# The feature tiles of the activations spread by 64 bytes each, in a two-layer hybrid decoder trunk on one core

## The reference

```
h    = rms_norm(x, norm_w[layer])
proj = einsum('bsd,de->bse', h, w_in[layer])        # 4096 -> 11792 columns
y    = concat(gla(...), swa(...), diff(...), rglru(...))   # four mixers of 1024 columns on slices of proj
y    = y * silu(gate)                               # gate: the last 4096 columns of proj
x    = x + einsum('bse,ed->bsd', y, w_out[layer])   # 4096 -> 4096
```

## Time and profile before

| | |
|---|---|
| time, median of 3 runs | 2979.4 us (2978.9 to 2979.46) |
| the profiled execution | 2979.48 us |
| its span | 2977.7 us |
| instructions | 37606 |
| PE (matmul) busy | 2938.4 us, 99% of the span |
| PEld (weight load) busy | 2479.5 us, 83% |
| DVE busy | 1604.9 us, 54% |
| ACT busy | 1458.0 us, 49% |
| bytes moved | 546.68 MB, mean 184 GB/s |

### The profile page before, as it was taken

One profiled execution on the slowest core, in us unless ns is written; L12 is line 12 of the kernel. 1 busy time (PEld: TensorE's weight loads), 2 busy tenths in 40 slices (PEclk: granted clock), 3 DMA queues, 4 the chain that ended last, 5 costly groups with the idle time before them and its releaser, 6 DMA issues.

```text
span 2977.7 us, 37606 instructions
## 1 busy us (share of the span) xinstructions
PE 2938.4 (99%) x14857; PEld 2479.5 (83%) x14857; DVE 1604.9 (54%) x2120; ACT 1458.0 (49%) x2059; POOL 52.0 (2%) x107
## 2 busy tenths in 40 slices
PE   8999999999999999999999999999999999999999
PEld 6888898888888898888878888988888888988887
DVE  5445455555666446444554455555556664554444
ACT  5344445555556545444554434445455665553333
POOL 2000000000000000000000000000000000000000
PEclk9999999999999999999999999999999999999999
DMA  7565556666655666666656655566666556666665
GB/s 223 175 187 161 163 164 174 185 186 181 178 163 162 185 177 190 217 214 203 212 176 191 184 157 169 160 184 181 181 179 177 162 167 180 183 200 207 219 219 168
DMA packets 281889, 546.68 MB, mean 184 GB/s; under 512 B 17688, under 2 KB 21920, under 8 KB 281712
## 3 DMA queue, kind: packets, MB, share of 16 engines
q1 hardware_dynamic: 271472, 524.88, 59.0%
q0 software_dynamic: 5552, 17.26, 1.9%
q10 hardware_dynamic: 4688, 2.13, 0.3%
HBM read 535.81 MB, written 8.39 MB: 183 GB/s over the span
## 4 chain that ended last, share of the span: by engine, by line
PE 98%; DMA 1%; ACT 1%; issue 1%; DVE 0%; ACTq 0%; PEldq 0%; DVEq 0%
PE main L1141 91%; PE mixer L1141 5%; DMA w_raw<-in_w_in 1%; ACT L385 0%; PE mixer L1355 0%; PE mixer L1200 0%; ACT stage L385 0%; PE mixer L1295 0%; PE mixer L1335 0%; PE mixer L1188 0%; DMA mix<-in_norm_w 0%; PE mixer L1322 0%; PE mixer L1285 0%; PE mixer L1323 0%; DVE w_lo L692 0%
## 5 line engine op out<-in xcount | busy, mean ns | idle before, releaser
L1141 PE MATMUL main<-w_hi,act 128*128 128x512 f32 x6912 | 2207.1, 394 | 26.7 <-PE main L1141 13.1
L692 DVE TENSOR_TENSOR w_lo<-w_raw,w_hi 128x1024 fp32r<-128x1024 f32 x992 | 1212.7, 1224 | 1238.8 <-PE main L1141 1004.8
L378 ACT ACTIVATE w_hi<-w_raw 128x1024 fp32r<-128x1024 f32 x992 | 1044.6, 1059 | 1099.5 <-PE main L1141 1076.0
L1141 PEld LDWEIGHTS main<-w_hi,act 128*128 128x128 f32 x6912 | 1299.7, 188 | 314.8 <-issue 39.1
L1141 PE MATMUL main<-w_lo,act 128*128 128x512 f32 x3456 | 1347.7, 390 | 0.0
L1141 PEld LDWEIGHTS main<-w_lo,act 128*128 128x128 f32 x3456 | 650.7, 188 | 129.2
L1141 PE MATMUL main<-act,w_hi 128*128 128x256 f32 x2048 | 377.2, 285 | 3.5 <-PE main L1141 1.8
L1141 PEld LDWEIGHTS main<-act,w_hi 128*128 128x128 f32 x2048 | 321.6, 192 | 6.2 <-issue 5.8
L1141 PE MATMUL main<-act,w_lo 128*128 128x256 f32 x1024 | 289.7, 283 | 0.0
L1141 PEld LDWEIGHTS main<-act,w_lo 128*128 128x128 f32 x1024 | 196.4, 192 | 0.2
L672 DVE SCALAR_TENSOR_TENSOR act<-act_T,par,act 128x256 fp32r<-128x256 f32 x96 | 42.0, 478 | 2.8 <-ACT act L360 2.5
(11 more groups left out here) (250 smaller groups left out, 1126.0 us busy)
## 6 DMA issues: line engine op xcount, KB each, us to landing
w_raw<-in_w_in SPq DMA_DIRECT2D x736, 512.0 KB, 3.6
w_raw<-in_w_out SPq DMA_DIRECT2D x256, 512.0 KB, 3.6
out<-mix POOLq DMA_DIRECT2D x15, 512.0 KB, 3.1
mix<-in_x POOLq DMA_DIRECT2D x8, 512.0 KB, 5.8
mix<-out POOLq DMA_DIRECT2D x8, 512.0 KB, 5.7
mix_Y<-in_x SPq DMA_DIRECT2D x3, 1024.0 KB, 16.3
mix_Y<-in_x SPq DMA_DIRECT2D x2, 512.0 KB, 4.8
act_T<-in_lru_w_r ACTq DMA_DIRECT2D x16, 64.0 KB, 2.0
```

The costliest lines, as they stand in the source:

```text
L378: act.activation(w_hi[:, n % HI, :, :], w_raw[:, n % RAW, :, :], ACT.Copy).then_inc(w_hi_ready, 1)
L692: dve.tensor_tensor(w_lo[:, n % LO, :, :], w_raw[:, n % RAW, :, :], w_hi[:, n % HI, :, :].bitcast(F32), ALU.subtract).then_inc(w_lo_ready, 1)
L1141: return pe.matmul(out_, lhsT, rhs, start=start, stop=stop, skip_group_check=True)
```

## The change

`act` gets feature tiles of 2 x 256 + 16 elements, 2112 bytes, of which the last 64 bytes are not used; `A` is a view of the rest with the same four indices as before, so no other line changes. `pad2` goes. After it, tile k begins at 18432 + 2112 k, `act_T` is at 42 x 2048 and `mix_Y` at 58 x 2048, and `w_raw`, `w_hi`, `w_lo` and all tiles behind them lie 128 bytes higher than before: `w_raw` at 151680, 74 x 2048 + 128.

```
         pad = sb("pad", [P, 56])
-        A = sb("act", [P, KT, 2, SEQ], F32R)
+        A_ROW = 2 * SEQ + 16
+        A = sb("act", [P, KT, A_ROW], F32R)[:, :, 0:2 * SEQ].rearrange("p k (q n) -> p k q n", q=2)
         F = sb("act_T", [P, KT * SEQ])
         YB = sb("mix_Y", [P, 6 * BW + HEADS * (SEQ + 4)])
-        pad2 = sb("pad2", [P, 480])
         w_raw = sb("w_raw", [P, RAW, KG, NC])
```

## The result

The changed kernel takes 3019.4 us (median of four runs, 3016.8 to 3021.0) against 2979.4, a ratio of 1.0134 with an interval of 1.0116 to 1.0151: 40 us slower. The forecast was 2979.4 with a range up to 3000, so the forecast and the range both missed. No engine has another instruction or another order; only addresses differ.

The account below looks back on a forecast made before the run. The prediction took PE's pace through the main matmuls to bound the kernel. Its terms for operand places, line crossings, ACT and DVE, and weight landing summed as 0 + 0 + 0 + 0, leaving 2979.4 us, range 2974 to 3000.

Parts of the forecast that it names:

- What bounds the kernel: Whole kernel: only PE's pace of main matmuls, or a feed so late that PE waits, could move the time.
- The remainder of 13.3 ns a matmul: Main matmuls: what is left of 226.7 ns wide and 120.0 narrow after one column a cycle, the same in both.
- How the two operands lie to each other: Main matmuls: stationary slice's address against the streamed one's, taken as zero, with ends of -13.3 and +4.3 ns.
- the low-rank projection: Nearest row with finer steps: stationary tile steps by 128 bytes, 231 ns a matmul, 4.3 ns above the main pace.
- The streamed row over a 2 KB line: Matmuls whose streamed row crosses a 2 KB line: taken as zero, upper end 11,808 x 4.3 ns = 51 us.
- The slower rival: All ordinary and half of turned chunks: line crossings cost PE time, 9.8 us (2989) to 51 us (3030); chance 0.17.
- The signs asked for in the prediction: PE's pace tile by tile: loss alike for all tiles means the streamed row, loss depending on k means the skew.
- The exception named there: Tiles k = 2, 10, 18 and 26 keep a 512-byte step against the weights, so a skew loss would spare them.
- ACT, DVE and the landing: Splits, act writers and weight transfers: zero each; splits stay 1059 and 1224 ns, no loss under a 6.9 us landing.
- The faster rival: Main matmuls: stationary load and stream stop colliding, 156 us saved, to 2823 us, or 2832 by the skill; chance 0.07.
- The range: Whole kernel: 2974 to 3000 us, holding the 0.75 for no change and crossings of up to 1.7 ns, about 0.1.

Follow-up runs that it names:

- e3_both128: Against the kernel before: everything from act on moved by 128 bytes together, tiles packed; 2980.1 us, ratio 1.0001.
- e10_matched: Against the kernel before: act tile k 64 x (k mod 4) bytes past a multiple of 256, its weight tiles at equal places; 3012.8 us, ratio 1.0113.
- e1_w128: Against the kernel before: act left packed, weights and all behind them moved to 128 bytes past a 2 KB line; 3024.9 us, ratio 1.0154.
- e9_turned64: Against the kernel before: in turned chunks only, w_hi and w_lo written and read 64 bytes further on; 2966.9 us, ratio 0.9959.
- e11_w64: Against the kernel before: act left packed, weights and all behind them moved to 64 bytes past a 2 KB line; 2985.0 us, ratio 1.0018.
- e5_fine_stairs: Against the kernel before: eight blocks of four act tiles at 16 to 240 bytes past a line, weights on 2 KB lines; 3017.9 us.
- e8_planes: Against the kernel before: act stored as two planes, high parts and low parts, without any gap, weights on 2 KB lines; 2979.9 us, ratio 0.9999.
- e12_step256: Against the kernel before: act tile k at 256 x (k mod 8) bytes past a 2 KB line, weights on 2 KB lines; 2979.4 us, ratio 0.9999.
- e4_stairs: Against the kernel before: four blocks of eight act tiles at 0, 64, 128 and 256 bytes past a line; 3004.1 us, ratio 1.0083.

## Why the prediction was wrong, point by point

**What bounds the kernel: right.** PE's pace was the only thing that could move it, and did. The remainder of 13.3 ns a matmul, read off the two paces, is the quantity that the places change: 13.3 ns over the streamed columns at place 0, 20 at place 64 in ordinary chunks (233.3), 6.7 in the best turned ones (113.3).

**How the two operands lie to each other: the step that failed.** "I take zero for this part" rested on a pace that is the same in all positions of the kernel before. But all of these are multiples of 512 bytes, and the effect has a period of 256: all rows of before, many as they are, showed one case. The only row with finer steps, the low-rank projection, showed 4.3 ns more, and I argued it away by its 32 columns. The price itself was in reach: 10,368 x 4.3 = 45 us, against the 40 measured. It stood at the end of the range of this step and was then given to no rival of its own, only lent to the crossing. What the runs show in place of the zero is a pace that depends on the two operands' places modulo 256 bytes: 5.0 ns more for a wide matmul and 1.2 less for a narrow one.

The low-rank row was also read a little high. Start by start, its two narrow matmuls take 0.26 us together and not 0.24, and the 31 wide ones are 230.0 ns apart, 230.8 in the second layer: 3.3 and 4.1 ns more than the main pace, or 34 and 43 us for 10,368. That these lie on both sides of 40 is partly chance, since the row has other places than the changed kernel. But in the kernel before its matmuls are already 224 to 239 ns apart in an uneven pattern, where the main ones keep 226 or 227, and a mean over 31 hid it. The row's stationary tile steps by 128 bytes in every run, so its slices never have one place, and it is above 226.7 in every run: 230.0 and 230.8 in e3_both128, 228.7 and 228.9 in the changed kernel. That is what one would expect if it is the same effect, but no run placed `wa` in steps of 256 bytes, so it isn't shown.

**The streamed row over a 2 KB line: right to cost it at zero.** e3_both128 shows it. The slower rival, with 0.17 of the chance, was this one, and it named the wrong mechanism; its 3030 at 4.3 ns came near by accident. The signs asked for in the prediction told them apart: it had a loss that depends on k for the skew, and the pattern over four tiles is there. The exception named there (none at k = 2, 10, 18, 26) isn't: the matmuls of tile 6, at an equal place modulo 256, are 228, 233 and 230 ns apart in chunk 28. The neighbours' places count as well, as e10_matched shows.

**ACT, DVE and the landing: right.** 1059, 1225, 495 and 478 ns, and 3.6 us to land with w_raw 128 bytes past a line. By the Trainium skill, "DMA: Bandwidth & Descriptors", section "How a descriptor splits into AXI transactions", an estimate of 3.8 us stood beside it; neither the changed kernel nor e1_w128 shows it, both at a median of 3.6.

**The faster rival: wrong sign, with something in it.** Equal places are the best for wide streams, not the worst. For narrow ones they are among the worst, and e9_turned64 takes 12.8 us from that. The rival's limit by the Trainium skill, "TensorE: Matmul & The Clock Gate", section "Wait — 56ns, not 53.3ns?", 215.7 ns for 512 columns, was reached at no place: 226.7 is the lowest of twelve.

**The range.** It stopped at 3000 with the slower case priced at up to 3030. The prediction gave 0.18 to that side and then left nearly half of it outside.

## What to carry to other kernels

A kernel that is bound by PE's pace, with a weight load for each matmul in float32r, should have the distance between its stationary and streamed tiles checked modulo 256 bytes, and every change of a tile's size ahead of them as well: here 16 bytes off cost up to 3% of a wide matmul's time in most chunks, and padding by multiples of 256 cost nothing. For narrow matmuls other places were better than equal ones, so the place is worth trying out for each kind. A pace that is equal at all positions proves nothing about positions that the kernel doesn't have; look first at the step between those that it has. When one row disagrees with the argument and its price can be multiplied out, that price deserves a rival of its own.

## What the runs showed of the hardware that was not expected

- With a weight load ahead of each matmul in float32r, the distance from one matmul to the next depends on the addresses of both operands modulo 256 bytes: 226.7 to 233.7 ns at 512 columns, 113.3 to 120.0 at 256. Moving both by 128 bytes changes nothing. The Trainium skill, "SBUF — State Buffer", section "SBUF: two separate sides", has PE's port wait for no one; that speaks of other engines, and the plain chunks of before agree (226 or 227 ns whether ACT and DVE work or not), but here the pace of PE depends on how its own two reads lie to each other. Whether they collide, or share some rhythm, no run shows.
- The sign turns between wide and narrow matmuls: equal places are best at 512 streamed columns and poor at 256. The two kinds also differ in which operand is stationary, and no run parts the one from the other.
- At place 192 the pace has two values, 113.3 or 117.8 ns narrow, 228.8 or 233.3 wide, and keeps the one that it has until the next interruption. Chunk 8 of e9_turned64 changes from 113.3 to 117.8 and back behind mixers' pieces. Which of the two it is doesn't look random: in e9_turned64 and e11_w64 the turned chunks have 17 stretches between interruptions in each layer, and each has the same value in the second layer as in the first, where the same work stands before it. Place 16 has two values as well (227.4 or 233.2 in e5_fine_stairs). So a stretch of stairs can show the value that the stretch ahead left behind, and the table above is a guide, not a law.
- What is compared with what inside PE stays open. The stream against its own slice, and the stream against the next one, are each excluded as the only rule; a common place of all slices and streams, which meets both conditions, was sufficient in all five kernels that had it in ordinary chunks throughout (the one before, e3_both128, e8_planes, e9_turned64, e12_step256), and in the two stretches of e4_stairs.
